# One inference step of a hybrid decoder on one core: the decode part and the sliding attention one weight chunk later

## The chip, the core and the metric

The kernel runs on one core of a Trainium2 chip. The metric is the device time of one execution in microseconds (us). Five engines work side by side, each through its own list of instructions in order: TensorE (PE: matmuls; PEld: its weight loads), VectorE (DVE), ScalarE (ACT), GpSimd (POOL) and SyncE (SP). They wait for each other on semaphores only. DMA transfers are issued from the lists of SP, ACT and POOL.

## The reference, cut to what matters

One layer of a decoder, for a prompt of 256 tokens and for 8 decode sequences of 4 tokens each (288 columns in all). The projection `w_in` gives the inputs of two parallel groups, an mLSTM with a short convolution ahead of it and a sliding-window attention with sinks; both go through `w_out`. A cross attention to 256 memory tokens and a squared-ReLU MLP follow.

```python
proj = h @ p['w_in']
qk_m, v_m, o_m, ig, fg, q_a, k_a, v_a = jnp.split(proj, idx, axis=-1)
qk_m, new_conv = causal_conv(qk_m, conv_buf, p['conv_w'], p['conv_b'])
...
h_m, C, n, m = mlstm_chunkwise(...)
...
if win_k is None:
    a_out = swa_prompt(q_a, k_a, v_a, p['sinks'], rel_bias)      # the prompt, windows of 128
else:
    a_out, new_k, new_v = swa_step(q_a, k_a, v_a, win_k, win_v, p['sinks'], rel_bias)   # decode
x = x + jnp.concatenate([h_m, a_out.astype(x.dtype)], axis=-1) @ p['w_out']
```

The attention has 16 heads of 64 and two key heads; scores get a relative bias and go through a softmax with a sink. Everything is float32.

## The kernel before

**The weight stream.** All weights come as 388 chunks of 512 KB (four row tiles of 128, 256 columns), in the order in which they are used, into a ring of four slots. SP issues the load of a chunk once the slot's old contents have been split. ScalarE rounds the chunk to fp32r (`whi`, 1.06 us), VectorE makes the rest (`wlo = raw - whi`, 1.2 us), and TensorE multiplies: three products (`whi` by the high half of the activations, `whi` by the low half, `wlo` by the high half), 24 matmuls of 288 columns, some 3.2 us a chunk. Four chunks make a group of two output tiles; the groups alternate between four PSUM banks `g`. After the fourth chunk of a group, VectorE evicts its two tiles (after chunks 27, 31, 35, 39, ...): tiles of the convolution's inputs go into `stage` with four small instructions each (`stage_conv`), the others with one multiplication by `rstd`. Value tiles use the same two `stage` buffers as the convolution tiles.

**The order beside the stream.** Everything else is hung onto chunks by hand, in a table `beside[c]` (L455 to L511) that all engines read. In step `c` TensorE multiplies chunk `c` and then does its part of each entry of `beside[c]`, in the order in which the entries stand. ScalarE and VectorE first split chunk `c + 3` and then do their parts; VectorE evicts behind them where `c % 4 == 3`. An engine that has no part in an entry passes over it. The entries of this stretch are:

- `dec_scores`, `dec_probs`, `dec_out`, `dec_turn`: the sliding attention of the decode tokens. Scores on TensorE, softmax on VectorE and ScalarE (`d_max`, `exps`, `softmax_sum`, product `dprob`), transposes, copies to SBUF (ScalarE `pTw`, VectorE `pTn` of 32x512), output, transposes, high and low halves.
- `swa_scores(t)`, `swa_exp(t)`, `swa_norm(t)`, `swa_probs(t)`, `swa_out(t)`, t = 0 to 7: the prompt's attention, two heads a step. TensorE's scores matmuls stand at list 33 + 3t beside the transposes of the step before; VectorE's scores (four SCALAR_TENSOR_TENSOR, two TENSOR_REDUCE, three small ones) in the same list; exponentials on ScalarE and the norm on VectorE one list on; the output matmuls, with the halves `a_hi` (ScalarE) and `a_lo` (VectorE), four lists on.
- `conv_taps(ct)` and `conv_gate(ct)`: the convolution of tile `ct`, at lists 32, 33, 40, 41, 48, 49, 56, 57 and two lists on; the last gate signals `conv_done` 8.
- `v_turn(i)`: TensorE transposes value tile `i` out of `stage`, which frees the buffer for the next convolution tile, and ScalarE copies it to `vm`. It waits for VectorE's maxima of an attention step (`V_AFTER`), since it uses that step's PSUM bank; `swa_scores(t)` for t = 2, 5, 7 waits for the copies (`V_BEFORE`).
- `m_expo`, `m_exps`, `m_zero`, `m_scores(h)`: the beginning of the mLSTM, from list 58 on.

**GpSimd's list** (L2250) runs beside the table with waits only. In this stretch it loads the bias tables of the attention steps and states of the mLSTM, and its last part reads:

```python
pool.wait_ge(sem["sc_mm"], 8)
c_load(1)
c_load(2)
pool.wait_ge(sem["av_mm"], 8)
pool.wait_ge(sem["a_lo"], 8)
row_load(1)
c_load(3)
pool.wait_ge(sem["conv_done"], 8)
pool.wait_ge(sem["prob_T"], 8)
copies(0)
```

`copies(0)` makes the fourfold copy of the decode keys (`k4`) that TensorE transposes in `m_scores(0)` (L723), behind that entry's first matmuls.

Of the kernel before, what the change touches and what calls it, by code (L numbers as in the profile page):

```python
# [218 lines left out]
def layer_kernel(nc, ins, outs, consts):  # L219
    with ExitStack() as ctx:  # L220
# [237 lines left out]
        beside = {c: [] for c in range(4 * WOUT + 5)}  # L458
# [6 lines left out]
            beside[10 + j].append(("x_squares", j))  # L465
        for c, what in ((12, "norm_x"), (12, "gates_mm"), (13, "gates_a"), (14, "gates_ln"), (15, "gates_b"),
                        (16, "gates_c"), (17, "keys_turn"), (17, "gates_exp"), (19, "keys_rev"), (20, "columns"),
                        (24, "mem_norm"), (30, "dec_scores"), (32, "dec_probs"), (33, "dec_out"),
                        (34, "dec_turn")):
            beside[c].append((what,))  # L470
        beside[15].append(("k_norm",))
        beside[22].append(("mem_squares",))
        for c, what in ((21, ("q_squares", 0)), (22, ("q_sums", 0)), (28, ("q_squares", 1)), (28, ("q_sums", 1)),
                        (29, ("q_root",)), (30, ("q_turn",))):
            beside[c].append(what)
        beside[30].reverse()
        for t in range(9):
            if t:
                beside[33 + 3 * t].append(("swa_probs", t - 1))
            if t < 8:  # L480
                beside[33 + 3 * t].append(("swa_scores", t))
                beside[34 + 3 * t] += [("swa_exp", t), ("swa_norm", t)]
            if t:
                beside[34 + 3 * t].append(("swa_out", t - 1))
        for ct in range(8):
            at = 4 * QKM + 4 + 8 * (ct // 2) + ct % 2
            beside[at].append(("conv_taps", ct))
            beside[at + 2].append(("conv_gate", ct))
        for g, c in enumerate((38, 46, 53, 60)):
            if g < 3:  # L490
                beside[c] += [("v_turn", 2 * g), ("v_turn", 2 * g + 1)]
        beside[58].append(("m_expo", 0))
# [1897 lines left out]
```

## Time and profile before

| | us |
|---|---|
| median of 3 runs | 1355.51 (1354.9 to 1355.52) |
| the profiled execution, device time | 1354.58 |
| its span in the profile | 1352.8 |
| TensorE busy | 1327.7 (98%) |
| VectorE busy | 818.2 (60%) |
| ScalarE busy | 620.9 (46%) |
| GpSimd busy | 98.6 (7%) |

The stretch that the diff touches lies between 118 and 250 us of the span. An engine's busy time counts its instructions; what matters for the time is where TensorE, the engine that is nearly always busy, has to wait. In a timeline each line is an instruction, or neighbours of one kind merged, with its start; idle time of the engine ahead of it stands in brackets with what ended it. The names `arena`, `small` and `m` are the shared working memory, the small columns and the PSUM banks beside the weight products.

### The profile page before, as it was taken

To read this page: it belongs to the slowest core of one execution; us is meant where nothing else is said; L and a number is where in the kernel's file an instruction comes from. 1 tells how busy PE (TensorE), PEld (TensorE's weight loads), DVE (VectorE), ACT (ScalarE), POOL (GpSimd) and SP (SyncE) were. 2 spreads that over 40 slices of the span, in tenths; PEclk is the share of its full clock that TensorE was granted. 3 is DMA by queue.
4 is the path that set the end of the run, shared out by engine and by line. 5 is a ranking of instruction groups with operands and counts; after the bars stand their busy time and mean duration, and the time that the engine had idled before them with its cause. 6 is when DMAs were issued, how large, how long until landed. Compare 5 with 4: busy or idle time off the path is not lost.

```text
span 1352.8 us, 27266 instructions
## 1 busy us (share of the span) xinstructions
PE 1327.7 (98%) x10213; PEld 1299.8 (96%) x10213; DVE 818.2 (60%) x1240; ACT 620.9 (46%) x889; POOL 98.6 (7%) x140
## 2 busy tenths in 40 slices
PE   7999999999999997999999999999999999999999
PEld 7998989988999987999999999999999999999999
DVE  7767888888756456656444556444565444565443
ACT  7674666666534456443333344333344333343331
POOL 0031001111523203000000000000000000000000
PEclk9999999999999999999999999999999999999999
DMA  9687445675955953654545555554555554555553
GB/s 380 254 228 253 134 140 184 193 232 166 368 180 158 299 203 110 218 158 156 183 159 166 167 161 155 178 164 160 168 164 159 171 170 156 169 158 168 171 160 127
DMA packets 75420, 251.87 MB, mean 186 GB/s; under 512 B 8348, under 2 KB 17392, under 8 KB 74704
## 3 DMA queue, kind: packets, MB, share of 16 engines
q1 hardware_dynamic: 59184, 215.49, 48.4%
q0 software_dynamic: 15888, 35.07, 8.4%
q8 instruction: 40, 0.66, 0.2%
q10 hardware_dynamic: 288, 0.48, 0.1%
q14 instruction: 20, 0.16, 0.0%
HBM read 238.00 MB, written 13.63 MB: 186 GB/s over the span
## 4 chain that ended last, share of the span: by engine, by line
PE 86%; DVE 6%; ACT 4%; issue 2%; DMA 2%; SPq 0%; DVEq 0%; ACTq 0%
PE g L521 81%; PE m L521 3%; DMA raw<-in_stream 2%; ACT arena L997 2%; DVE wlo L1476 1%; DVE arena L1462 1%; ACT whi L1015 1%; DVE arena L1459 1%; DVE b_lo L1462 0%; ACT a_hi L997 0%; DMA arena<-in_memT 0%; DVE arena L1451 0%; DVE arena L1455 0%; DVE small L1742 0%; PE m L746 0%
## 5 line engine op out<-in xcount | busy, mean ns | idle before, releaser
L1476 DVE TENSOR_TENSOR wlo<-raw,whi 128x1024 fp32r<-128x1024 f32 x388 | 475.5, 1235 | 371.4 <-ACT whi L1015 359.9
L1015 ACT ACTIVATE whi<-raw 128x1024 fp32r<-128x1024 f32 x388 | 407.4, 1058 | 471.3 <-PE g L521 440.7
L521 PE MATMUL g<-a_hi,whi 128*128 128x288 f32 x1632 | 353.5, 298 | 1.5 <-ACT a_hi L997 1.5
L521 PE MATMUL g<-a_hi,wlo 128*128 128x288 f32 x1632 | 350.2, 296 | 0.0
L521 PE MATMUL g<-a_lo,whi 128*128 128x288 f32 x1632 | 348.7, 295 | 0.0
L521 PE MATMUL g<-b_hi,whi 128*128 128x288 f32 x1344 | 287.8, 295 | 5.5 <-DVE arena L1459 5.3
L521 PE MATMUL g<-b_hi,wlo 128*128 128x288 f32 x1344 | 289.0, 296 | 0.0
L521 PE MATMUL g<-b_lo,whi 128*128 128x288 f32 x1344 | 287.0, 295 | 0.0
L521 PEld LDWEIGHTS g<-a_hi,whi 128*128 128x128 f32 x1632 | 261.7, 188 | 7.6 <-issue 4.0
L521 PEld LDWEIGHTS g<-a_lo,whi 128*128 128x128 f32 x1632 | 261.9, 188 | 0.0
L521 PEld LDWEIGHTS g<-a_hi,wlo 128*128 128x128 f32 x1632 | 261.5, 188 | 0.0
L521 PEld LDWEIGHTS g<-b_hi,whi 128*128 128x128 f32 x1344 | 216.1, 188 | 7.8 <-DVE wlo L1476 6.6
L521 PEld LDWEIGHTS g<-b_lo,whi 128*128 128x128 f32 x1344 | 215.7, 188 | 0.0
L521 PEld LDWEIGHTS g<-b_hi,wlo 128*128 128x128 f32 x1344 | 215.4, 188 | 0.0
L997 ACT ACTIVATE b_hi<-arena 128x288 f32 (+1 forms) x72 | 32.0, 445 | 108.4 <-DVE arena L1462 100.1
L1459 DVE TENSOR_TENSOR arena<-arena,g 128x288 f32 (+1 forms) x96 | 43.5, 453 | 49.3 <-PE g L521 43.2
L521 PE MATMUL m<-arena 128*64 128x128 f32 (+14 forms) x608 | 56.9, 332 | 1.9 <-DVE arena L1451 1.4
L521 PEld LDWEIGHTS m<-arena 128*32 128x32 f32 (+6 forms) x608 | 38.3, 140 | 14.4 <-issue 9.5
L997 ACT ACTIVATE a_hi<-arena,gcol 128x288 fp32r<-128x288 f32 (+1 forms) x48 | 25.6, 534 | 39.6 <-DVE arena L1459 37.2
L1462 DVE SCALAR_TENSOR_TENSOR arena<-g,rstd 128x288 f32<-128x288 f32 x64 | 29.2, 457 | 24.0 <-PE g L521 22.8
L1459 DVE TENSOR_TENSOR b_lo<-arena,b_hi 128x288 f32 (+1 forms) x72 | 33.0, 458 | 16.4 <-ACT b_hi L997 7.8
L997 ACT ACTIVATE arena<-arena 128x288 f32<-128x288 f32 (+9 forms) x65 | 36.6, 564 | 12.4 <-DVE arena L1462 7.0
(181 smaller groups left out, 690.9 us busy)
## 6 DMA issues: line engine op xcount, KB each, us to landing
raw<-in_stream SPq DMA_DIRECT2D x388, 512.0 KB, 3.5
arena<-in_state_C POOLq DMA_DIRECT2D x8, 512.0 KB, 5.8
out_s_C<-arena POOLq DMA_DIRECT2D x8, 512.0 KB, 3.5
arena<-in_kdT POOLq DMA_DIRECT2D x8, 512.0 KB, 15.0
arena<-in_cache_mem_v POOLq DMA_DIRECT2D x8, 512.0 KB, 8.7
arena<-in_xT SPq DMA_DIRECT2D x4, 576.0 KB, 8.4
arena<-in_memT SPq DMA_DIRECT2D x4, 512.0 KB, 7.0
arena<-in_x_prompt SPq DMA_DIRECT2D x2, 1024.0 KB, 10.0
```

What stands on the lines that cost most here:

```text
L521: return pe.matmul(out, lhsT, rhs, start=start, stop=stop, skip_group_check=True)
L997: return act.activation(out, in_, func, **kw)
L1015: act.activation(whi[:, s], raw[:, s], ACT.Copy).then_inc(sem["hi_done"], 1)
L1459: return dve.tensor_tensor(out, a, b, op)
L1462: return dve.scalar_tensor_tensor(out=out, in0=a, scalar=s, in1=b, op0=op0, op1=op1)
L1476: dve.tensor_tensor(wlo[:, s], raw[:, s], f32(whi[:, s]), SUB).then_inc(sem["chunk_split"], 1)
```

## The change

The four decode entries, all eight steps of the prompt's attention and the turns of the value tiles 0 to 5 move to the next chunk's list: the decode entries from 30, 32, 33, 34 to 31, 33, 34, 35, scores of step t from 33 + 3t to 34 + 3t, what follows them likewise, and the value turns from 38, 46, 53 to 39, 47, 54. The query turn stays in list 30, so the reversal of that list's order falls away. The turns of value tiles 6 and 7, the convolution, the evictions, the mLSTM and GpSimd's list stay where they are.

```diff
-                        (24, "mem_norm"), (30, "dec_scores"), (32, "dec_probs"), (33, "dec_out"),
-                        (34, "dec_turn")):
+                        (24, "mem_norm"), (31, "dec_scores"), (33, "dec_probs"), (34, "dec_out"),
+                        (35, "dec_turn")):
             beside[c].append((what,))
...
-        beside[30].reverse()
         for t in range(9):
             if t:
-                beside[33 + 3 * t].append(("swa_probs", t - 1))
+                beside[34 + 3 * t].append(("swa_probs", t - 1))
             if t < 8:
-                beside[33 + 3 * t].append(("swa_scores", t))
-                beside[34 + 3 * t] += [("swa_exp", t), ("swa_norm", t)]
+                beside[34 + 3 * t].append(("swa_scores", t))
+                beside[35 + 3 * t] += [("swa_exp", t), ("swa_norm", t)]
             if t:
-                beside[34 + 3 * t].append(("swa_out", t - 1))
+                beside[35 + 3 * t].append(("swa_out", t - 1))
...
-        for g, c in enumerate((38, 46, 53, 60)):
+        for g, c in enumerate((39, 47, 54, 60)):
             if g < 3:
                 beside[c] += [("v_turn", 2 * g), ("v_turn", 2 * g + 1)]
```

## Rows read from the trace of the kernel before

**Rows 1.** The page: busy time of TensorE, and its clock in 40 slices.
```profile
PE 1327.7 (98%) x10213; PEld 1299.8 (96%) x10213; DVE 818.2 (60%) x1240; ACT 620.9 (46%) x889; POOL 98.6 (7%) x140
...
PEclk9999999999999999999999999999999999999999
```

**Rows 2.** TensorE's timeline, 118 to 192 us: start, length, engine, line, instruction.
```profile
119.27 1.14 PE L521 MATMUL m<-arena 64*32 64x128 f32 x64 [0.50 <-DVE arena L1451]
...
127.64 0.33 PE L647 MATMUL m<-cst,arena 128*128 128x128 f32 x1 [0.67 <-DVE arena L1459]
...
132.79 2.90 PE L521 MATMUL m<-arena 128*32 128x64 f32 x72 [0.88 <-DVE arena L1451]
...
159.44 0.93 PE L521 MATMUL m<-arena 64*128 64x256 f32 x8
...
171.98 0.93 PE L521 MATMUL m<-arena 64*128 64x256 f32 x8
...
184.58 0.63 PE L694 MATMUL m<-cst,arena 128*128 128x128 f32 x4 [0.65 <-DVE b_lo L1459]
...
191.91 0.85 PE L720 MATMUL m<-cst,arena 128*128 128x128 f32 x6 [1.16 <-DVE small L1459]
```

**Rows 3.** VectorE's timeline in the decode part.
```profile
121.08 1.02 DVE L1462 SCALAR_TENSOR_TENSOR arena<-m,arena 128x320 f32<-128x320 f32 x2
...
126.76 0.82 DVE L1459 TENSOR_TENSOR arena<-arena,small 128x640 f32<-128x640 f32 x1
...
131.97 0.67 DVE L1451 COPY arena<-m 32x512 f32<-32x512 f32 x1
132.68 1.93 DVE L1462 SCALAR_TENSOR_TENSOR arena<-arena,gcol 128x312 f32<-128x312 f32 x4
```

**Rows 4.** VectorE's timeline in attention steps 1 to 3.
```profile
155.97 0.16 DVE L1459 TENSOR_TENSOR small<-small 128x4 f32<-128x4 f32 x1 [1.57 <-ACT small L997]
...
158.03 1.23 DVE L1476 TENSOR_TENSOR wlo<-raw,whi 128x1024 fp32r<-128x1024 f32 x1
...
161.00 1.77 DVE L1462 SCALAR_TENSOR_TENSOR arena<-m,small,arena 128x256 f32<-128x256 f32 x4
...
164.61 0.06 DVE L1915 MEMSET arena<- 128x3 f32 x1
...
166.63 1.22 DVE L1476 TENSOR_TENSOR wlo<-raw,whi 128x1024 fp32r<-128x1024 f32 x1
...
176.03 1.77 DVE L1462 SCALAR_TENSOR_TENSOR arena<-m,small,arena 128x256 f32<-128x256 f32 x4
```

**Rows 5.** Timeline of VectorE, GpSimd and TensorE, 244 to 250 us.
```profile
244.67 0.41 DVE L1459 TENSOR_TENSOR b_lo<-m,b_hi 128x256 fp32r<-128x256 f32 x1
...
245.65 0.55 POOL L2180 DMA_DIRECT2D arena<-rows_scratch  x1 [17.46 <-DVE b_lo L1459]
...
246.19 0.75 POOL L2180 DMA_DIRECT2D arena<-in_state_C  x1
...
247.94 0.45 DVE L1462 SCALAR_TENSOR_TENSOR arena<-arena 128x288 f32<-128x288 f32 x1
...
248.45 0.29 POOL L2233 COPY arena<-arena 128x128 f32<-128x128 f32 x1 [1.51 <-DVE arena L1462]
...
248.75 0.99 PE L521 MATMUL m<-arena 128*128 128x256 f32 x6
...
249.67 0.55 PE L738 MATMUL m<-cst,arena 128*128 128x128 f32 x3
```

**Rows 6.** TensorE's timeline where it starts, and at its longest later gap.
```profile
7.81 0.77 PE L521 MATMUL g<-whi,b_hi 128*128 128x256 f32 x2 [7.81 <-ACT b_hi L997]
...
11.71 0.40 PE L521 MATMUL g<-whi,b_hi 128*128 128x256 f32 x2
11.95 0.40 PE L521 MATMUL g<-whi,b_lo 128*128 128x256 f32 x2
...
50.63 0.72 PE L521 MATMUL m<-arena,cst 128*128 128x288 f32 x2 [2.05 <-DVE arena L1455]
```

## The prediction

> **What bounds the kernel now.** I read the page first: TensorE is busy 98% of the span, and the row of its clock is flat [rows 1]. So the time is the work of TensorE plus its gaps, and a change that moves work without adding any can only act through gaps. The list of waits gives the gaps with their releasers; the timeline of TensorE shows the five that lie in the stretch that the diff touches, as idle time in brackets [rows 2]: 0.50 us before the decode scores, 0.67 before the decode probabilities, 0.88 before the decode output, 0.65 before the probabilities of step 3, 1.16 before the turns of value tiles 2 and 3. Sum: 3.86 us, 0.28% of the time. That is the ceiling of what the change can give. Every one ends with VectorE, so the third reading is VectorE's timeline in the same stretch, then GpSimd's, whose queue hangs on these steps.
>
> **What the change does.** No instruction is added or removed. Each engine's list keeps its work; the decode entries, the attention entries and the value turns stand one chunk later, while the splits, the evictions of finished tiles (after chunks 31, 35, 39, ...), the convolution taps (32, 33, 40, 41, ...) and the conv gates stay. A chunk is 3.2 us of TensorE. What is gained or lost is which VectorE work lies between a producer and TensorE's need. Costs of VectorE's blocks, each from the start of its first instruction to the start of what follows: split 1.15, attention scores 3.6, taps of one tile 1.97, eviction of two conv tiles 2.02 [rows 3, 4]; norm with the low half of the output 2.06 (155.97 to 158.03). After a scores block VectorE waits for ScalarE's exponentials: 1.57 idle behind a 1.23 split, so 2.8 from the end of scores to norm, 6.4 from the start of scores.
>
> **Decode scores, one chunk later.** TensorE waited 0.50 for the query copies. One chunk more is 3.2 us: the wait goes. Minus 0.50.
>
> **Decode probabilities.** From the end of the scores' matmuls (119.27 + 1.14) TensorE needs 6.56 us for its two chunks (up to 127.64 less 0.67). VectorE needs 6.5 from the start of the scores (121.08) to the end of the product (126.76 + 0.82), and it started 0.67 late, because it came from the query turn. One chunk later it is free in time. The 0.67 shrinks to 0 to 0.1; I take 0.1.
>
> **Decode output: a larger wait in place of the small one.** Between the end of the product (127.58) and the copy that TensorE waits for (131.97) VectorE does a split, the eviction after chunk 31 and a split [rows 3]: 1.15 + 2.02 + 1.15 fill the 4.4 us. In the new order the split of list 31 comes before the scores, but that of list 33 is added, and so are the taps of list 32: the copy now stands behind eviction, split, taps, split. Net one block of 1.96 more, while TensorE's own distance (decode probabilities and one chunk) is the same. The wait becomes 0.88 + 1.96 = 2.84. Bounds: 0.88 if something delays TensorE equally, 3.3 if ScalarE's split is late too.
>
> **Steps 0 to 7.** The old stalls come from a pile-up: from scores 2 (161.00) VectorE works without a gap to scores 3 (176.03), 15.0 us, with two evictions, both taps and four splits between, where TensorE needs 12.54 (159.44 to 171.98). Hence the 0.65 at step 3, and the 1.16 behind it. In the new order the eviction falls before scores 2, so the way is 3.6 + 1.97 + 1.15 + 2.06 + 1.97 + 1.15 + 0.5 + 1.15 = 13.5. TensorE asks for probabilities 10.9 us after the matmuls of its scores (12.54 less 1.6 for the matmuls of the pair). I carry VectorE's lateness at each scores block on. After the decode wait step 0 starts 0.2 late, step 1 1.6 (decode turn, eviction), step 2 1.2, step 3 2.1. Step 3 then needs 6.4 + 2.06 = 8.4, ready at 10.5 against 10.9: no wait. Step 4 starts 0.3 late (8.4 + 2.3 = 10.7 of VectorE against 12.5); its maximum is ready at 3.9 and the value turns ask at 4.5 (one chunk, one output): the 1.16 goes. Between scores 4 and 5 lie now 6.4 + 2.06 + 0.2 (ones) + 2.02 + 1.15 + 1.97 + 1.15 = 15.0 against 13.1: step 5 starts 2.0 to 2.2 late. Its norm has to follow taps as well: 3.6 + 1.97 + 1.15 + 2.06 = 8.8, ready at 10.8 to 11.0 against 10.9. That is the tightest place; I take 0.1, bounds 0 and 0.5. Step 6 starts 2.5 late and has 11.5 (value turns 4 and 5 lie in between); step 7 is on time.
>
> **Value turns.** Those of tiles 0 and 1 now stand at the chunk whose eviction reuses their staging buffers, so VectorE waits for TensorE's turn, under 0.6 us, which the slack of step 2 covers. No cost.
>
> **GpSimd's queue.** The last low half (step 7, list 59 in place of 58) releases a row load and the load of a state quarter; behind them stands the copy of the keys for which the first mLSTM scores wait. Before, the half ended at 245.08, the loads were issued by 246.94 and the copy waited for the convolution (248.39) [rows 5]. Now the half ends just ahead of the last conv gate. From scores 7 VectorE has 3.6 + 2.02 + 1.15 + 2.06 + 1.97 + 1.15 + 1.97 + 1.15 = 15.1, and gate, exponents, split and half, which in their old order take 3.3 (244.67 to 247.94): 18.4 to the half's end. TensorE has 10.9 (three chunks and an output), 0.6 of transposes, two chunks of 3.2 and the last output of 1.2, so 19.1 to 19.2 to its mLSTM scores. The half is 0.8 ahead. GpSimd needs from there 0.57 + 0.54 + 0.75 + 0.29 = 2.15, so the copy ends 1.35 after TensorE starts those scores, and TensorE asks for it at 0.92 (248.75 to 249.67). New wait: 0.4; bounds 0 and 1.0. The loads are wanted one head later and are hidden.
>
> **Sum.** -3.86 + 2.84 + 0.1 + 0.1 + 0.4 = -0.4 us. The profiled execution took 1354.58 (span 1352.8, 1.8 around it), 0.93 under the median of 1355.51. So 1354.2 in its terms, **1355.1 us** in the median's. Ends: -3.86 + 0.88 and nothing else new gives 1352.5; -3.86 + 3.3 + 0.1 + 0.5 + 1.0 gives 1356.6. The likeliest case's own range is 1353.6 to 1356.4.
>
> **Rivals.**
> - The clock of TensorE falls in the 2.84 us wait. At the start of the program it idles 7.81 us and then runs nine pairs of matmuls in 3.90 us that later take 0.24 each (11.71 to 11.95), 2.15 in all: the engine is at 1.2 and not 2.4 GHz, and 1.75 us are lost, though the page's clock row shows no fall. After an idle time of 2.05 us, at 50.63, nothing of the kind is seen [rows 6]. 2.84 lies between, nearer the second. 1355.1 + 1.75 = 1356.8. Chance 0.12. The Trainium skill has this as a rule ("TensorE: Matmul & The Clock Gate", section "Why this matters for your kernels"): gaps between bursts of matmuls cost the full clock. By that rule the time would be this rival's.
> - GpSimd's key copy is held by VectorE's split, which would run beside it now: one split, 1.2 us more, 1356.3. The old copy ran beside no split and took 0.29. Chance 0.05. The Trainium skill ("SBUF — State Buffer", section "Who interferes with whom") says that a VectorE instruction with two SBUF inputs and a GpSimd instruction that reads SBUF exclude each other; no row here shows it.
> - The change does what a shift ought to: all five waits go, and ScalarE or VectorE reaches the decode copy in time. 1355.5 - 3.9 = 1351.6. For it: four of the five do go. Against it: the count of blocks in front of the copy. Chance 0.08.
> - Slower than before: VectorE falls behind in steps 3 to 6. My sum has it 2.1 late at scores 5, where a wait begins. If ScalarE's halves of the splits come late there and each of four steps costs VectorE 1 us more, it is 6 late, TensorE waits 3.5 to 4 in all: 1358.6. It decides from 3 us more lateness than I count. Against it: VectorE's idle times are in these sums already, and a wait of TensorE gives VectorE the time back. Chance 0.05.
>
> **How the numbers follow.** The forecast has 0.70. About 0.2% (2.7 us) is what a measurement of this kernel can tell from no change; 1352.8 to 1358.2 is within it. Forecast, clock and key copy are inside, 0.87; faster 0.08; slower 0.05. The range leaves out the two outer rivals and the thin end of the low bound, and takes in the clock: 1353.2 to 1357.1.
>
> **What would show it.** After: no wait before the decode scores; one of 2.5 to 3.1 us before the decode output, released by the 32x512 copy; none before the probabilities of step 3 and the value turns; 0 to 0.5 before those of step 5; some 0.4 before the fourth transpose of the first mLSTM head, released by GpSimd. A matmul pace of 0.43 per pair behind the decode output would be the clock. A decode wait under 1.5 us makes the prediction wrong on the fast side, any wait over 1 us in steps 1 to 7 on the slow side.

## The result, and the profile after

| | before | after |
|---|---|---|
| median of 16 runs, us | 1354.86 | 1357.12 |
| lowest, us | 1353.83 | 1355.71 |
| ratio | | 1.0018 (95%: 1.001 to 1.0026) |
| profiled execution, us (span) | 1354.58 (1352.8) | 1357.23 (1355.4) |
| mean granted clock in it | 1.0 | 0.997 |

The change makes the kernel slower by 0.18%, 2.3 us. One execution of each kernel, of about three times the length (4206.85 and 4155.79), is left out of the ratio. The forecast was 0.4 us less than before. 1357.12 lies just outside the range (1353.2 to 1357.1); set against the 1355.51 from which the forecast started, that range is -2.3 to +1.6 us, and +2.3 was measured. The two profiled executions are 2.65 us apart.

The page of the changed kernel, its lines for TensorE and its clock:

```profile
PE 1330.9 (98%) x10213; PEld 1302.5 (96%) x10213; DVE 818.5 (60%) x1240; ACT 621.6 (46%) x889; POOL 98.6 (7%) x140
...
PEclk9999899999999999999999999999999999999999
```

Against [rows 1] TensorE is busy for 3.2 us more (1327.7 to 1330.9) with the same 10213 instructions, and the clock row has an 8 in its fifth slice of 34 us, which is 136 to 169 us. So the time doesn't lie in idle time: the same work takes longer.

TensorE's waits in the changed kernel, 110 to 262 us (engine, line waited at, releaser: sum, times, longest):

```profile
PE m L520 <- DVE arena L1450: 2.8, 1, 2.8
PE m L737 <- POOL arena L2232: 0.5, 1, 0.5
PE m L520 <- DVE arena L1461: 0.2, 1, 0.2
```

Four of the five waits of [rows 2] are gone, the one before the decode output has grown from 0.88 to 2.82, and two stand at the first mLSTM scores. VectorE's timeline behind the decode probabilities says where the first comes from:

```profile
128.76 0.82 DVE L1458 TENSOR_TENSOR arena<-arena,small 128x640 f32<-128x640 f32 x1
129.66 0.06 DVE L1914 MEMSET arena<- 128x3 f32 x1
...
131.68 1.23 DVE L1475 TENSOR_TENSOR wlo<-raw,whi 128x1024 fp32r<-128x1024 f32 x1
...
132.82 1.92 DVE L1461 SCALAR_TENSOR_TENSOR arena<-arena,gcol 128x312 f32<-128x312 f32 x4
...
134.78 1.23 DVE L1475 TENSOR_TENSOR wlo<-raw,whi 128x1024 fp32r<-128x1024 f32 x1
...
135.92 0.67 DVE L1450 COPY arena<-m 32x512 f32<-32x512 f32 x1
```

Product (to 129.58), eviction, split, taps, split, copy: from the product's end to the copy's start are 6.34 us, in [rows 3] 4.39 (127.58 to 131.97). The difference, 1.95, is the taps. TensorE's timeline in the changed kernel:

```profile
118.39 0.38 PE L599 MATMUL m<-cst,arena 128*128 128x128 f32 x2
...
121.89 1.16 PE L520 MATMUL m<-arena 64*32 64x128 f32 x64
...
129.64 0.33 PE L646 MATMUL m<-cst,arena 128*128 128x128 f32 x1
...
136.74 3.88 PE L520 MATMUL m<-arena 128*32 128x64 f32 x72 [2.82 <-DVE arena L1450]
140.54 0.85 PE L520 MATMUL g<-a_hi,whi 128*128 128x288 f32 x2
141.19 0.68 PE L520 MATMUL g<-a_lo,whi 128*128 128x288 f32 x2
...
145.02 0.43 PE L520 MATMUL g<-a_hi,whi 128*128 128x288 f32 x2
145.29 0.43 PE L520 MATMUL g<-a_lo,whi 128*128 128x288 f32 x2
...
145.82 0.38 PE L668 MATMUL m<-cst,arena 128*128 128x128 f32 x2
...
216.49 0.63 PE L693 MATMUL m<-cst,arena 128*128 128x128 f32 x4
...
250.94 1.07 PE L520 MATMUL m<-arena 128*128 128x256 f32 x6 [0.23 <-DVE arena L1461]
...
252.50 0.55 PE L737 MATMUL m<-cst,arena 128*128 128x128 f32 x3 [0.50 <-POOL arena L2232]
...
256.73 0.59 PE L520 MATMUL m<-arena 128*128 128x257 f32 x2
```

The 72 matmuls at the decode output (64 of its own, then 8 of the scores of step 0) take 3.88 us and not the 2.90 of [rows 2]. Nearly all pairs of the chunk behind them take 0.68 to 0.85 in the records and stand 0.48 apart; the last three, from 145.02 on, take 0.43 and stand 0.27 apart. The windows of the changed kernel show it as a clock (us, busy time and count of TensorE, its weight loads, VectorE, ScalarE, GpSimd; granted clock; DMA share; GB/s):

```profile
130.00:136.00 6.00, 3.92 (x31) 3.65 (x29) 5.62 (x13) 4.77 (x9) 0.00 (x0) 1.00 0.26 87
136.00:138.00 2.00, 1.26 (x44) 0.84 (x45) 1.89 (x5) 0.00 (x0) 0.00 (x0) 1.00 0.40 86
138.00:139.00 1.00, 1.00 (x30) 0.57 (x26) 0.93 (x3) 0.00 (x0) 0.00 (x0) 0.59 0.82 328
139.00:145.00 6.00, 6.00 (x30) 5.62 (x27) 4.80 (x12) 1.88 (x3) 0.48 (x1) 0.50 0.28 94
145.00:150.00 5.00, 5.00 (x39) 5.00 (x39) 2.13 (x5) 3.49 (x13) 0.27 (x1) 1.00 0.62 157
```

A clock of 1.00 is 2.4 GHz and one of 0.50 is 1.2 GHz, the lower level. The clock is still 1.00 up to 138, 1.3 us behind the end of the wait at 136.74; the 0.59 of the next microsecond says that it falls at about 138.2, and it is back at 145.0. So some 6.8 us run at 1.2 GHz: the last third of the 72 matmuls and three quarters of the chunk. For the account two rows of the kernel before are wanted that stand with those of [rows 2] in TensorE's timeline, the decode turn and the first mLSTM norm:

```profile
138.91 0.38 PE L669 MATMUL m<-cst,arena 128*128 128x128 f32 x2
...
253.90 0.81 PE L521 MATMUL m<-arena 128*128 128x257 f32 x3
```

The query turn starts at 118.39 in both kernels. From there to the mLSTM norm are 135.51 us before and 138.34 after, 2.83 more. From the decode output to the decode turn, the stretch that holds the lower clock, are 6.12 us before (132.79 to 138.91) and 9.08 after (136.74 to 145.82): 2.96 more, 0.98 of it in the output's matmuls and 1.98 in the rest. All that is left, waits included, is -0.13. **Between these two profiled executions the waits balance, and the clock is the whole loss.**

### The profile page after: what moved, and what is told of

Read it like the earlier page. It is cut to its first block, busy times and chain, and to the rows that moved or that the text cites. A ratio compares the mean times of both kernels' runs of the same rounds, so it can differ in the third digit from the quotient of the medians.

```text
span 1355.4 us, 27268 instructions
## 1 busy us (share of the span) xinstructions
PE 1330.9 (98%) x10213; PEld 1302.5 (96%) x10213; DVE 818.5 (60%) x1240; ACT 621.6 (46%) x889; POOL 98.6 (7%) x140
## 4 chain that ended last, share of the span: by engine, by line
PE 89%; DVE 5%; ACT 3%; issue 2%; DMA 2%; POOL 0%; SPq 0%; DVEq 0%; ACTq 0%; POOLq 0%
PE g L520 84%; PE m L520 4%; DMA raw<-in_stream 1%; DVE wlo L1475 1%; ACT arena L996 1%; ACT whi L1014 1%; DVE arena L1461 1%; DVE arena L1458 1%; DVE b_lo L1461 0%; ACT a_hi L996 0%; DMA arena<-in_memT 0%; DVE arena L1454 0%; PE m L693 0%; PE m L745 0%; ACT b_hi L996 0%
```

## Experiments

The kernel before ran beside each of them on the same chip: 1354.6, 1354.63 and 1354.32 us in the three groups. The first four of the list are one group, the next four another, the last three the third.

### taps_behind: the changed kernel with the taps of tile 0 behind the decode copy

```diff
-            beside[at].append(("conv_taps", ct))
+            beside[at if ct else 33].append(("conv_taps", ct))
```

> The changed kernel, with the taps of convolution tile 0 moved from list 32 to list 33, behind the decode probabilities. Clock theory (the wait before the decode output is one VectorE block longer, 2.82 us, and TensorE runs at half clock for about 8 us after it, some 3 us lost): the wait falls back to 0.9, all matmuls behind it keep their 0.27 us pace, the later steps get waits of 0.5 to 1 us in sum because VectorE has the taps still to do; 3.5 to 4.5 us below the changed kernel, 1.0 to 2.0 us below the kernel before. Wait-alone theory (the slow pace has another cause, such as the transfers or what runs beside it): only about 1.5 us below the changed kernel, half pace still seen. Shift theory (the shifted steps themselves cost the time): no change against the changed kernel.

1353.35 us (1353.07 to 1354.17, 11 runs), ratio 0.9991 (0.9982 to 1.0): 3.8 below the changed kernel, or 3.5 if each is set against the kernel before beside it. TensorE's timeline in it:

```profile
134.53 2.90 PE L520 MATMUL m<-arena 128*32 128x64 f32 x72 [0.86 <-DVE arena L1450]
137.37 0.54 PE L520 MATMUL g<-a_hi,whi 128*128 128x288 f32 x2
137.74 0.43 PE L520 MATMUL g<-a_lo,whi 128*128 128x288 f32 x2
```

One entry of 1.96 us moved takes the wait from 2.82 to 0.86 and the output back to 2.90, and the pairs behind it are at full pace at once. The time falls by the 1.96 and by 1.5 to 1.8 more, though small waits come up behind it (0.22 to 0.29 at steps 0 and 3). The place of the loss is shown.

### taps_ahead_before: the kernel before with the same taps ahead of its decode copy

```diff
+        beside[32].reverse()
```

> The kernel before, with nothing shifted, only the taps of tile 0 put ahead of the decode probabilities within list 32. Clock theory: the wait before the decode output goes from 0.88 to about 2.84 and is followed by 8 us of matmuls at half pace; 4.5 to 5 us above the kernel before, though no entry is in another list. Wait-alone theory: 2.0 us above, full pace. Shift theory: within 2 us above, since no step is shifted; half pace not seen.

1358.75 us (1357.15 to 1359.91, 8 runs), ratio 1.0029 (1.0019 to 1.004), 4.15 more than before. TensorE's timeline and the windows of this kernel:

```profile
134.79 4.39 PE L522 MATMUL m<-arena 128*32 128x64 f32 x72 [2.85 <-DVE arena L1452]
```

```profile
130.00:134.00 4.00, 1.94 (x15) 1.71 (x13) 3.76 (x9) 2.58 (x5) 0.00 (x0) 1.00 0.57 173
136.00:142.00 6.00, 6.00 (x57) 4.89 (x53) 2.58 (x6) 2.52 (x5) 0.00 (x0) 0.50 0.26 87
142.00:150.00 8.00, 8.00 (x62) 8.00 (x62) 6.46 (x18) 5.52 (x17) 0.75 (x1) 1.00 0.33 100
```

Nothing of the shift is in this kernel, and both the wait (2.85) and the fall of the clock (0.50 from 136 to 142) are. So the order of taps and copy makes them, whatever else moves. The sum is a little under the 4.5 to 5 expected.

### decode_back: the steps one chunk later, the decode entries where they were

```diff
-                        (24, "mem_norm"), (31, "dec_scores"), (33, "dec_probs"), (34, "dec_out"),
-                        (35, "dec_turn")):
+                        (24, "mem_norm"), (30, "dec_scores"), (32, "dec_probs"), (33, "dec_out"),
+                        (34, "dec_turn")):
...
+        beside[30].reverse()
```

> The changed kernel with the four decode entries in their old lists (30, 32, 33, 34) and the attention steps and value turns in the new ones. Clock theory: waits of 0.50, 0.67 and 0.88 in the decode part as before, none before the probabilities of step 3 and the value turns, 0.2 to 0.5 before the key transposes; full pace throughout; 1.0 to 1.6 us below the kernel before. Shift theory: 1 to 3 us above the kernel before.

1354.58 us (1354.07 to 1356.55, 11 runs), ratio 1.0002 (0.9993 to 1.0011). The decode waits of before are back (0.35, 0.68, 0.87), that at step 3 is smaller (0.20), that at the value turns is gone, and the end of the sliding attention has waits of its own. TensorE's timeline at the first mLSTM head:

```profile
247.82 1.07 PE L521 MATMUL m<-arena 128*128 128x256 f32 x6 [0.21 <-DVE arena L1462]
...
249.39 0.55 PE L738 MATMUL m<-cst,arena 128*128 128x128 f32 x3 [0.49 <-POOL arena L2233]
```

Summed by distances between the same instructions, TensorE waits 3.98 us in this stretch and 4.09 in the kernel before: the shift of the steps alone is worth nothing that can be measured. I had expected more than a microsecond from it; what the steps gain is paid at the first mLSTM scores.

### keys_first: GpSimd copies the keys before it issues the row and state loads

```diff
+            pool.wait_ge(sem["conv_done"], 8)
+            pool.wait_ge(sem["prob_T"], 8)
+            copies(0)
             pool.wait_ge(sem["av_mm"], 8)
             pool.wait_ge(sem["a_lo"], 8)
             row_load(1)
             c_load(3)
-            pool.wait_ge(sem["conv_done"], 8)
-            pool.wait_ge(sem["prob_T"], 8)
-            copies(0)
```

> The changed kernel with GpSimd's key copy put ahead of the row load and the state load instead of behind them. If the 0.50 us wait before the key transposes comes from those two loads, it goes and the time falls by 0.5 us against the changed kernel, 2.82 us of wait and the half pace stay. If the copy is held by a VectorE split beside it, a wait of 0.3 to 1 us stays.

1357.57 us (1355.5 to 1359.84, 10 runs), ratio 1.0022 (1.0013 to 1.0032): no gain, where 0.5 was expected. TensorE's timeline behind the first mLSTM scores in it:

```profile
251.95 0.55 PE L737 MATMUL m<-cst,arena 128*128 128x128 f32 x3
...
264.92 0.72 PE L520 MATMUL m<-arena 32*128 32x257 f32 x8 [1.48 <-DMA arena<-arena]
```

The fourth transpose no longer waits, so the two loads in GpSimd's queue were the cause of the 0.50. Thirteen microseconds on there is a wait of 1.48 for a transfer within the working memory, which ScalarE issues: it lands 7.7 us after its issue, 5.7 in the kernel before and 6.1 in the changed one. That the state load, which now comes later, delays it was not tested by itself.

### copy_on_act: the changed kernel with the decode copy on ScalarE

ScalarE makes the copy behind its own copy from the same bank, TensorE waits for ScalarE at both places that use it, and VectorE's entry goes.

```diff
+                A(pTn, M[1][0:32, :].rearrange("p (a b) -> p a b", a=4)).then_inc(sem["act_once"], 1)
+                act.wait_ge(sem["act_once"], now("dpn_out"))
...
-                pe.wait_ge(sem["dve_once"], before["dpn_out"] + 1)
+                pe.wait_ge(sem["act_once"], before["dpn_out"] + 1)
...
-            def dec_probs():
-                dve.wait_ge(sem["pe_once"], before["dprob_T"] + 1)
-                copy(pTn, M[1][0:32, :].rearrange("p (a b) -> p a b", a=4)).then_inc(sem["dve_once"], 1)
-                dve.wait_ge(sem["dve_once"], now("dpn_out"))
```

> The changed kernel with the 32x512 copy of the decode probabilities done by ScalarE, behind its own copy, instead of VectorE; the lists of beside are those of the change. Clock theory: ScalarE has both copies done 2 us before TensorE gets to the decode output, so the 2.82 us wait goes and no matmul runs at half pace; VectorE's lateness against TensorE grows by the time that TensorE gains, so waits of 0.3 to 1 us appear before the probabilities of steps 0, 3 and 5; 4 us below the changed kernel, 1 to 2 us below the kernel before. If the decode output waits for something else, it keeps a wait of over 1 us.

1352.55 us (1352.06 to 1353.73, 11 runs), ratio 0.9984 (0.9975 to 0.9994): faster than both kernels, 4.6 below the changed one and 2.1 below the one before. Four rows of TensorE's timeline in it, between 50 and 138 us:

```profile
50.57 0.72 PE L520 MATMUL m<-arena,cst 128*128 128x288 f32 x2 [2.43 <-DVE arena L1456]
...
54.59 0.44 PE L520 MATMUL m<-a_hi,wgx 128*128 128x288 f32 x1
...
56.64 0.30 PE L520 MATMUL m<-a_hi,wgx 128*128 128x288 f32 x1
...
135.24 2.90 PE L520 MATMUL m<-arena 128*32 128x64 f32 x72 [0.21 <-ACT arena L996]
```

The decode wait is 0.21 and the output has its 2.90. The first line is a surprise. At 50 us, far from the change, this execution waits 2.43 us, and 13 matmuls from 51.71 on stand 0.24 apart where later ones stand 0.13 to 0.14 apart. From the end of that wait to the next weight chunk are 6.34 us, 4.80 in the kernel before: 1.54 lost. Its windows:

```profile
52.00:55.00 3.00, 3.00 (x14) 3.00 (x14) 1.74 (x1) 2.21 (x3) 0.00 (x0) 0.50 0.42 158
55.00:60.00 5.00, 5.00 (x40) 5.00 (x39) 4.72 (x10) 0.00 (x0) 0.00 (x0) 1.00 0.27 79
```

It is the wait of 2.05 in [rows 6], on which the prediction rested its view of the clock, a little longer in this execution, and here the clock falls.

### gap_two, gap_three, gap_four: the wait alone, in three lengths

taps_behind with two, three or four small memsets on VectorE ahead of the decode copy. They fill a spare buffer; nothing of the computation is changed.

```diff
                 dve.wait_ge(sem["pe_once"], before["dprob_T"] + 1)
+                for _ in range(2):
+                    dve.memset(nsq[:, :], 0.0).then_inc(sem["dve_step"], 1)
+                    dve.wait_ge(sem["dve_step"], now())
```

> The kernel with the taps behind the probabilities (0.86 us wait before the decode output), with two memsets of 288 columns on VectorE ahead of the copy that TensorE waits for. The wait grows to 1.5 to 1.7 us. If the fall of the clock needs a wait as long as that of the change, every matmul keeps its pace and the time is 0.7 us above taps_behind.

> The same with three memsets: a wait of 1.9 to 2.1 us before the decode output, as long as the wait of 2.05 at 50 us that is followed by full pace in the kernel before. Clock theory with the length of the wait alone deciding: full pace, 1.1 us above taps_behind. If what ran before the wait decides too, half pace may be seen and the time is 3 to 4 us above taps_behind.

> The same with four memsets: a wait of 2.3 to 2.5 us. If this length is enough for the clock, half pace for 7 to 8 us and 4 to 4.5 us above taps_behind; if not, 1.5 us above it.

The decode output in the timelines of the three:

```profile
136.95 4.38 PE L520 MATMUL m<-arena 128*32 128x64 f32 x72 [1.71 <-DVE arena L1450]
```

```profile
135.98 3.68 PE L520 MATMUL m<-arena 128*32 128x64 f32 x72 [2.14 <-DVE arena L1450]
```

```profile
136.32 4.05 PE L520 MATMUL m<-arena 128*32 128x64 f32 x72 [2.57 <-DVE arena L1450]
```

In these profiled executions the output took 4.38, 3.68 and 4.05 us in place of 2.90, so the clock fell in each of the three, behind 1.71 us too. In gap_two and gap_four it is low for some 6.8 us, as in the changed kernel, and in gap_three for half of that:

```profile
138.00:141.00 3.00, 3.00 (x18) 2.61 (x15) 2.86 (x6) 1.88 (x3) 0.00 (x0) 0.50 0.01 3
142.00:146.00 4.00, 4.00 (x33) 4.00 (x32) 3.72 (x9) 1.79 (x7) 0.75 (x1) 1.00 0.40 135
```

From the output to the decode turn, 6.12 us at full clock, gap_three takes 7.65 and the other two take 8.91 and 9.03: the short fall costs 1.5 us and the long one 2.8 to 3.0. A mean clock of 0.997 or less over the whole execution stands for the lower level for some 7 us in all, one of 0.998 or 0.999 for less. The wait in the table is that of the profiled execution.

| kernel | wait, us | median, us (runs) | ratio | mean clock of 0.997 or less | mean clock of 1.0 |
|---|---|---|---|---|---|
| copy_on_act | 0.21 | 1352.55 (11) | 0.9984 | 0 of 11 | 8 of 11 |
| taps_behind | 0.86 | 1353.35 (11) | 0.9991 | 0 of 11 | 9 of 11 |
| gap_two | 1.71 | 1354.74 (10) | 1.0001 (0.9991 to 1.001) | 4 of 10 | 4 of 10 |
| gap_three | 2.14 | 1355.59 (10) | 1.0006 (0.9996 to 1.0015) | 5 of 10 | 1 of 10 |
| gap_four | 2.57 | 1356.49 (10) | 1.0009 (1.0 to 1.0018) | 7 of 10 | 0 of 10 |
| changed kernel | 2.82 | 1357.12 (15) | 1.0018 | 14 of 15 | 0 of 15 |
| changed_again | 2.83 | 1356.51 (11) | 1.0014 | 6 of 11 | 0 of 11 |
| keys_first | 2.82 | 1357.57 (10) | 1.0022 | 9 of 10 | 0 of 10 |
| taps_ahead_before | 2.85 | 1358.75 (8) | 1.0029 | 6 of 8 | 0 of 8 |

The kernel before, with its 0.88, has a mean clock of 0.997 or less in 2 of the 89 executions of the three groups and of 1.0 in 51.

From taps_behind to gap_four the wait grows by 1.71 us and the median by 3.14: the remaining 1.4 is clock. Against taps_behind the three are 1.4, 2.2 and 3.1 us longer, each between what was expected with and without the fall (0.7 without it for gap_two; 1.1 without and 3 to 4 with it for gap_three; 1.5 and 4 to 4.5 for gap_four): a median over executions with and without a long fall. Within gap_two the four executions at a mean clock of 1.0 took 1353.75 to 1354.13, the four at 0.996 and 0.997 took 1355.67 to 1357.31. So no single length parts the two: behind 1.71 us the same kernel keeps the clock or loses it. But from 2.57 us on not one of 54 executions has a mean clock of 1.0. The 12 of them at 0.998 and 0.999 can have a short fall at the decode output, or one at the wait of 50 us alone; the records of the timed executions don't tell which. If they had kept the clock at the decode output, about half of them or more should be at 1.0, as behind the waits of 0.21 to 0.88. None is, so most of them probably fell there too, for less time, as the profiled execution of gap_three did (0.999). That is argued: none of the 12 was profiled.

### before_copy_on_act, copy_on_act_keys_first, changed_again: what the shift is worth without its wait

The kernel before with the copy on ScalarE; copy_on_act with the key copy of keys_first; the changed kernel once more.

> The kernel before with ScalarE doing the 32x512 copy. The 0.88 us wait before the decode output goes, the waits of 0.65 and 1.16 in the attention steps stay: 0.5 to 0.9 us below the kernel before. Set beside copy_on_act it tells what the shift is worth once its own wait is taken away: if the clock was all that the shift cost, the shifted kernel is 0.5 to 1.5 us the faster of the two; if the shift has another cost, the two are equal or the shifted one is slower.

> copy_on_act with the key copy put ahead of GpSimd's two loads. If the wait before the key transposes is worth what the profile shows, 0.5 us below copy_on_act. If the loads, now issued 0.5 us later, meet the transfers that the first state matmuls need, as the wait of 1.48 us for a DMA in keys_first suggests, the gain is lost: within 0.3 us of copy_on_act or up to 1 us above it.

> The changed kernel on the same chip as the two others. 2 to 3 us above the kernel before; nearly every execution with a mean clock of 0.996 or 0.997.

| kernel | median, us (11 runs each) | ratio |
|---|---|---|
| before_copy_on_act | 1353.82 | 0.9995 (0.9986 to 1.0004) |
| copy_on_act_keys_first | 1352.62 | 0.9985 (0.9976 to 0.9994) |
| changed_again | 1356.51 | 1.0014 (1.0005 to 1.0023) |

With the copy on ScalarE in both, the shifted kernel (here with the key copy ahead as well) is 1.2 us below the unshifted one (1352.62 against 1353.82). Without the key copy the ratio was 0.9984, in another group. The intervals of the two ratios overlap, so this is a difference of medians and not a settled one. The key copy moved ahead adds nothing again: TensorE's timeline of copy_on_act_keys_first has the transfer's wait in its place:

```profile
259.19 0.72 PE L520 MATMUL m<-arena 32*128 32x257 f32 x8 [0.57 <-DMA arena<-arena]
```

changed_again is slower than before on this chip as well. Six of its 11 executions have a mean clock of 0.997 and took 1356.51 to 1357.46, one has 0.998 (1356.35), four have 0.999 and took 1355.52 to 1355.95.

## Why the prediction was wrong, step by step

**The step that failed** is the price of the decode wait: the sum has 2.84 for its length and nothing for the clock behind it. The clock stood in the first rival alone, "The clock of TensorE falls in the 2.84 us wait", with a chance of 0.12, because "2.84 lies between, nearer the second", and a price of 1.75. In the changed kernel it is the rule: all 15 executions have a mean clock under 1.0, 14 of them 0.997 or less, and in the profiled one it costs 2.96. Both halves came from [rows 6]. The price was read from nine pairs at the program's start, at the lower clock for 3.9 us; here it was low for 6.8 us. The chance was read from one execution in which a wait of 2.05 did no harm. In other executions that same wait was 2.37 (gap_two) and 2.43 (copy_on_act), and the clock fell behind both. The kernel before may have this in its own executions: in the first group 15 of its 29 have a mean clock of 1.0 and took 1353.53 to 1354.6, 14 have 0.998 or 0.999 and took 1354.93 to 1355.61, about 1.2 us more. That was not seen in a trace of it. The Trainium skill ("TensorE: Matmul & The Clock Gate", section "Why this matters for your kernels") says that an idle gap between bursts of matmuls costs the full clock. The trace agrees that it does, with 2.82 us idle and a clock of 0.50 behind it; but the Trainium skill speaks of longer gaps there than any in this part of the kernel, and here the clock fell behind 1.71 us too, so the measurement decides.

With the measured terms the account of the profiled executions closes to 0.2 us: 1354.58 - 0.13 + 2.96 = 1357.41 against 1357.23. From the medians it closes to 0.6: 1354.86 - 0.13 + 2.96 = 1357.7 against 1357.12. Executions in which the clock is lower for less time than in the profiled one, such as the one at 1355.71 (mean clock 0.999), would give that difference; this was not seen in a trace.

**The decode wait** was right: 2.84 forecast, 2.82 measured, and released by the 32x512 copy. taps_behind shows that it is the taps.

**The decode scores and probabilities** were right: no wait ahead of the scores (121.89), none ahead of the probabilities (129.64), where the sum had 0.1.

**Steps 0 to 7** were right: the 0.65 and the 1.16 are gone, and step 5 is the tight place as forecast. From the scores to its probabilities are 7.68 us where 7.56 would be without a wait (the row at 216.49), so 0.12 against 0.1.

**The first mLSTM scores** were mis-sized: 0.4 forecast, 1.04 measured. GpSimd and VectorE in the changed kernel, 249 to 253 us:

```profile
249.88 0.42 DVE L1458 TENSOR_TENSOR b_lo<-m,b_hi 128x256 fp32r<-128x256 f32 x1
...
250.34 0.46 DVE L1461 SCALAR_TENSOR_TENSOR arena<-arena 128x288 f32<-128x288 f32 x1
...
250.87 0.55 POOL L2179 DMA_DIRECT2D arena<-rows_scratch  x1 [17.68 <-DVE b_lo L1458]
...
251.41 0.75 POOL L2179 DMA_DIRECT2D arena<-in_state_C  x1
...
252.15 0.30 POOL L2232 COPY arena<-arena 128x128 f32<-128x128 f32 x1
```

The chain itself is the forecast one: the half ends at 250.30, the copy at 252.45, 2.15 as worked out. But the last conv gate was about 0.6 later than my sum of VectorE's blocks had it. The scores need that gate and start 0.40 late, by distances (4.76 from the start of the last attention output, where an output and one chunk take 4.36 elsewhere), and from their start to the transposes are 1.56 us in place of 0.92, 0.64 more. I had priced only the second.

**The list of what goes** was too short by 0.2: by distances the old waits are 4.09, not 3.86. So the waits come to -4.09 + 2.82 + 0.12 + 1.04 = -0.11, with -0.13 measured where I had -0.4.

**The other rivals.** The key copy was not held by a split: it took 0.30, in [rows 5] 0.29, and VectorE's split began at 252.45, when it was done, so whether the two exclude each other was not put to the test. All waits going (1351.6) did not come; copy_on_act comes near it (1352.55), by giving the copy to another engine. VectorE didn't fall behind in steps 3 to 6.

## What to carry to other kernels

Where TensorE is the bound, price a new wait as its length and as what the clock costs behind it, and look for that price in how the next matmuls stand apart, not only in idle time. One execution in which a wait did no harm doesn't show that it is harmless: compare the wait and the clock over many. Here a wait of 2.82 us cost up to 3 us more behind it. And before a block of work is moved past a small copy, ask whether an engine that is free there can take the copy, which here turned the same shift from 0.18% slower to 0.16% faster.

## What the runs showed of the hardware

- TensorE's clock falls behind waits of 1.71 us too, and not in every execution. A mean clock of 0.997 or less, some 7 us at 1.2 GHz, comes in none of 22 executions after 0.21 and 0.86, in 4 of 10 after 1.71, 5 of 10 after 2.14, 7 of 10 after 2.57 and 35 of 44 after 2.82 to 2.85. A mean clock of 1.0 comes in 17 of 22, 4 of 10, 1 of 10, 0 of 10 and 0 of 44.
- At the wait of 50 us the profiled executions had no fall after 1.21 to 2.16 us (eleven of them) and a fall after both 2.37 and 2.43. The same wait of the same kernel differs from one execution to the next: 1.91 and 1.76 in two of the changed kernel.
- The fall comes not with the end of the wait but behind it, when TensorE is busy again: 1.4 us behind in the changed kernel, where the first 48 of the 72 matmuls still ran at full pace, and 0.4 us behind in taps_ahead_before (the 4.39 us of its output in place of 3.88).
- The cost goes by how long the clock is low and not by the length of the wait: 1.5 us in gap_three behind 2.14 and in copy_on_act behind 2.43 (low for some 3.4 us), 2.8 to 3.0 in gap_two behind 1.71 and in the changed kernel behind 2.82 (some 6.8 us).
- GpSimd's issue of the two loads took 0.55 and 0.75 us, and 0.57 passed from VectorE's last write to the first of them. Behind such a queue a copy of 0.30 is ready 2.15 us after its release.
